# A decoder layer on one core: 32 of 44 feed-forward up steps as seven block products

## The reference

```python
D_MODEL = 1024; SEQ = 512; D_FF = 2816

def swiglu(x, w_gu, w_down):
    g, u = jnp.split(x @ w_gu, 2, axis=-1)
    return (jax.nn.silu(g) * u) @ w_down

def reference(x, ...):
    x = x + 0.5 * rms_norm(swiglu(rms_norm(x, ffn1_norm_pre), ffn1_w_gu, ffn1_w_down), ffn1_norm_post)
    h = rms_norm(x, mix_norm_pre)
    ...                                  # two attention mixers, gates, output projection
    x = x + rms_norm(merged @ w_out, mix_norm_post)
    x = x + 0.5 * rms_norm(swiglu(rms_norm(x, ffn2_norm_pre), ffn2_w_gu, ffn2_w_down), ffn2_norm_post)
```

## Time and profile before

| what | value |
|---|---|
| median of three executions | 1206.68 us (1205.62 to 1207.15) |
| the profiled execution | 1207.43 us, its span 1205.7 us |
| granted TensorE clock | 1.00, of full speed, in each of the 40 slices 0.9 or more |
| PE matmul busy | 1188.7 us, 99% of the span |
| PE weight loads busy | 986.2 us, 82% |
| DVE busy | 535.2 us, 44% |
| ACT busy | 399.0 us, 33% |
| POOL busy | 86.8 us, 7% |
| up steps (two feed-forwards) on the chain of waits | 53% with the gate and projection steps of the same line |
| down steps on the chain | 20% |

### The profile page before, as it was taken

The page is one execution under the profiler, slowest core; times in us unless marked ns, Lnnn a source line. Parts: engine busy times, 40 slices in busy tenths (PEclk is TensorE's granted clock), DMA queues, the critical chain, the costliest instruction groups (busy, mean ns, idle before and its releaser), DMA issues.

```text
span 1205.7 us, 15537 instructions
## 1 busy us (share of the span) xinstructions
PE 1188.7 (99%) x6054; PEld 986.2 (82%) x6054; DVE 535.2 (44%) x806; ACT 399.0 (33%) x643; POOL 86.8 (7%) x198
## 2 busy tenths in 40 slices
PE   9999999999999999999999999999999999999998
PEld 7888888888887888998777788887888888888886
DVE  3444444431226435436776343646444444442223
ACT  5222222221125211246676313325422222221113
POOL 7000000000005100000031100002000000000002
PEclk9999999999999999999999999999999999999999
DMA  7843333232225343371200232332333333333321
GB/s 207 263 113 96 104 104 87 87 123 105 105 87 145 96 118 104 108 242 36 73 3 2 70 105 70 123 105 70 101 90 88 104 104 96 83 115 107 105 70 70
DMA packets 138511, 123.19 MB, mean 102 GB/s; under 512 B 4180, under 2 KB 125180, under 8 KB 138444
## 3 DMA queue, kind: packets, MB, share of 16 engines
q1 hardware_dynamic: 134272, 108.02, 29.7%
q0 software_dynamic: 4080, 14.50, 3.7%
q10 hardware_dynamic: 112, 0.03, 0.0%
HBM read 118.08 MB, written 8.90 MB: 105 GB/s over the span
## 4 chain that ended last, share of the span: by engine, by line
PE 93%; DVE 2%; DMA 2%; ACT 1%; issue 1%; SPq 0%; DVEq 0%; ACTq 0%
PE ps L1369 53%; PE ps L1453 20%; PE ps L1556 4%; PE ps L1824 4%; PE ps L1622 2%; PE ps L1611 2%; DMA ring_raw<-in_ffn_w_gu 2%; PE ps L1808 2%; PE ps L1679 2%; PE ps L1657 1%; PE ps L1796 1%; PE ps L1393 1%; ACT ring_hi L670 1%; DVE ring_lo L946 1%; DMA x_tok<-in_x 0%
## 5 line engine op out<-in xcount | busy, mean ns | idle before, releaser
L1369 PE MATMUL ps<-xn_hi,ring_hi 128*128 128x512 f32 x992 | 388.7, 392 | 2.9 <-DVE ring_lo L946 1.6
L1369 PE MATMUL ps<-xn_hi,ring_lo 128*128 128x512 f32 x992 | 386.2, 389 | 0.0
L1369 PE MATMUL ps<-xn_lo,ring_hi 128*128 128x512 f32 x992 | 386.1, 389 | 0.0
L946 DVE TENSOR_TENSOR ring_lo<-ring_raw,ring_hi 128x2048 fp32r<-128x2048 f32 (+1 forms) x89 | 201.8, 2268 | 255.5 <-ACT ring_hi L670 255.5
L670 ACT ACTIVATE ring_hi<-ring_raw 128x2048 fp32r<-128x2048 f32 (+1 forms) x89 | 167.9, 1888 | 255.1 <-PE ps L1453 157.6
L1369 PEld LDWEIGHTS ps<-xn_hi,ring_hi 128*128 128x128 f32 x992 | 186.2, 188 | 42.7 <-issue 4.3
L1369 PEld LDWEIGHTS ps<-xn_hi,ring_lo 128*128 128x128 f32 x992 | 186.2, 188 | 39.1
L1369 PEld LDWEIGHTS ps<-xn_lo,ring_hi 128*128 128x128 f32 x992 | 186.3, 188 | 37.7
L1453 PE MATMUL ps<-ring_hi,hT_hi 128*128 128x512 f32 x352 | 136.9, 389 | 0.0
L1453 PE MATMUL ps<-ring_hi,hT_lo 128*128 128x512 f32 x352 | 136.9, 389 | 0.0
L1453 PE MATMUL ps<-ring_lo,hT_hi 128*128 128x512 f32 x352 | 136.9, 389 | 0.0
(11 more groups left out here) (232 smaller groups left out, 1161.6 us busy)
## 6 DMA issues: line engine op xcount, KB each, us to landing
ring_raw<-in_ffn_w_gu SPq DMA_DIRECT2D x86, 512.0 KB, 5.0
ring_raw<-in_ffn_w_down SPq DMA_DIRECT2D x44, 512.0 KB, 4.0
ring_raw<-in_w_in SPq DMA_DIRECT2D x44, 512.0 KB, 4.7
ring_raw<-in_w_out SPq DMA_DIRECT2D x8, 512.0 KB, 4.3
bias_rows_sparse<-bias_by_distance POOLq DMA_DIRECT2D x1, 2560.0 KB, 15.5
x_tok<-in_x SPq DMA_DIRECT2D x8, 256.0 KB, 5.3
ring_raw<-in_cmp_w_k SPq DMA_DIRECT2D x4, 512.0 KB, 4.4
ring_raw<-in_cmp_w_v SPq DMA_DIRECT2D x4, 512.0 KB, 4.5
```

Source lines behind the costliest of these rows:

```text
L946: e = dve.tensor_tensor(dst, src, f32(r), ALU.subtract)
L1369: e = pe.matmul(ps[:, 2 * (slot if pair is None else pair) + c, :], part(a, slot, k * 256 + c * P, P), xn[b][:, k, :], start=(k == 0 and i ...
```

## The change

In each feed-forward the first 6 up steps (`CLASSIC`) stay as they are. The other 16 (`MIXED`) are computed with Strassen's identity in Winograd's form: the weight step is four blocks B11, B12, B21, B22 (halves of K and the g and u columns), the normed x four blocks (halves of K and of the tokens), and seven block products take the place of eight. A block product is 4 slices of K x 3 matmuls of 128x128 by 128x256, 84 matmuls in a step instead of 48 of 128x512.

- **Weight side.** POOL forms four sums of blocks per step, 128x512 each: T3 = B22 - B12, T2 = T3 + B11, T1 = B12 - B11, T4 = B21 - T2 (`mix_weights`). ACT and DVE make high and low parts of seven blocks of 128x512 (`hi_block`, `lo_block`) instead of one of 128x2048, in the order B11, T2, T1, T3, B21, T4, B22. The slots are those of `ring_hi` and `ring_lo`, in 512-wide pieces; T1 and T4 are formed in the place of their own low parts.
- **x side**, once per feed-forward: POOL joins the high and low parts of x (`join_x`, four of 128x1024), DVE scales the four by `rb` (`norm_x`) and forms s1 and s3 (`mix_x`), POOL forms s2 and x12 - s2 (its own `mix_x`, called inside the first `mix_weights`, behind T3 and T2). ACT and DVE make seven high and low parts of 128x1024 (`hi_mixed`, `lo_mixed`). All of it stands between the steps 0 to 6 in the queues. The low part of x11 and of s1 may only be written when s2 has been formed.
- **Result side.** Three PSUM banks per step, alternately two sets, into which several products accumulate. ACT copies the first product to `s1`; DVE adds `s1` to the second bank after product 1 (`t_part`), after product 3 (`u_part`) and after product 5 (the u or g part of the second token half), and forms the other corners from them: 128x256 each. These sums stand ahead of the low parts that follow them in DVE's queue. PE waits for `t_part` before product 3, for `s1` before product 4, for `u_part` before product 5 and for the sum c22 before product 6.
- **h** is kept in fp32 (`hT`); its high part (`h_hi`, four slots) and low part, in the place of h itself, are made two steps of h at a time in the down stage (`hi_h`, `lo_h`, 128x1024), the first ones in the last two block steps.
- **POOL's queue.** The bias tables are built after the first feed-forward's up steps (`w_used` at 22) instead of at the start.

The diff, cut to its core:

```diff
+CLASSIC = 6
+MIXED = UP - CLASSIC
+SOURCES = ("B11", "T2", "T1", "T3", "B21", "T4", "B22")
...
+            def join_x(f):
+                pool.wait_ge(*xlo_event(2 * f, KD - 1))
+                for dst, ks, t0 in ((x_21[:, :, :], 0, 256), (x_22[:, :, :], 4, 256), (x_sum[0][:, :, :], 0, 0), (x_sum[4][:, :, :], 4, 0)):
...
+            def mix_weights(f, i, u, between=None):
...
+                pool.wait_ge(raw_loaded[u % 2], raw_count(f, i, u))
+                if not (isinstance(i, int) and 2 * i + u == 0):
+                    pool.wait_ge(blk_lo, of_step(f, i, u - 1, 6, 4))
+                pool.tensor_tensor(t3, b22, b12, ALU.subtract).then_inc(t_ready, 1)
+                pool.wait_ge(t_ready, of_step(f, i, u, 4, 1))
+                pool.tensor_tensor(t2, t3, b11, ALU.add).then_inc(t_ready, 1)
+                if between:
+                    between()
+                pool.wait_ge(*block_free(f, i, u, 2))
+                pool.tensor_tensor(t_sum(f, 2), b12, b11, ALU.subtract).then_inc(t_ready, 1)
+                pool.wait_ge(*block_free(f, i, u, 5))
+                pool.wait_ge(t_ready, of_step(f, i, u, 4, 2))
+                pool.tensor_tensor(t_sum(f, 5), b21, t2, ALU.subtract).then_inc(t_ready, 1)
...
+                mix_weights(f, 0, 0, lambda: mix_x(f))
...
+                def lo_mixed(b):
+                    if b in (0, 2):
+                        dve.wait_ge(x_mixed2, 2 * f + 1)
...
+                def mixed(i, u, last=False, late=lambda: None):
...
+                    dve.wait_ge(blk_used, of_step(f, i, u, 6, 2))
+                    dve.wait_ge(s1_ready, of_step(f, i, u, 1, 1))
+                    dve.tensor_tensor(t_part[:, :], y, s1[:, v, :], ALU.add).then_inc(t_taken, 1)
+                    late()
+                    for b in range(2):
+                        following(b)
...
+                    dve.tensor_tensor(u_part[:, :], y, s1[:, v, :], ALU.add).then_inc(u_taken, 1)
+                    dve.wait_ge(u_taken, of_step(f, i, u, 1, 1))
+                    dve.tensor_tensor(h_f32[:, v, 256:512], z, u_part[:, :], ALU.add).then_inc(c22_taken, 1)
...
+                    for b in range(2, 5):
+                        following(b)
...
+                    dve.tensor_tensor(hT[:, at_j], silu_g[:, v, :], h_f32[:, v, :], ALU.mult).then_inc(h_ready, 1)
+                    for b in (5, 6):
+                        following(b)
...
+                        if b == 3:
+                            pe.wait_ge(t_taken, of_step(f, i, u, 1, 1))
...
+                        for k in range(4):
+                            for q, (a, x) in enumerate(MODES):
+                                e = pe.matmul(ps[:, bank, 0:256], block_at(a, f, b)[:, k * P:(k + 1) * P], (x_hi, x_lo)[x][b][:, k, :],
```

More of the change, by code:

```diff
@@ new lines, in mix @@
+            def mix(f):
+                join_x(f)
+                mix_weights(f, 0, 0, lambda: mix_x(f))
+                mix_weights(f, 0, 1)
+                with pool.Fori(1, MIXED // 2) as i:
+                    for u in range(2):
+                        mix_weights(f, i, u)
+                pool.wait_ge(up_scaled, CLASSIC * (f + 1))
+            mix(0)
+            load_gain(g1_post)
+            pool.wait_ge(w_used, UP)
+            pool.memset(bias_vec[0:20, :], MASKED).then_inc(vec_filled, 1)
@@ L742, in ffn, with rest @@
                     root()
-                for u in range(2):
-                    up(0, u)
-                with act.Fori(1, UP // 2) as i:
-                    for u in range(2):
-                        up(i, u)
-                n = base + UP + 2
-                hi(0, n)
-                with act.Fori(0, (DOWN - 3) // 2) as i:
-                    for u in range(1, 3):
-                        hi(i, n + u)
+                for n in range(2):
+                    silu(n)
+                hi(0, base + 3)
+                for b in (3, 0, 2):
+                    hi_mixed(b)
+                silu(2)
+                hi(0, base + 4)
+                for b in (1, 4):
+                    hi_mixed(b)
+                silu(3)
+                hi(0, base + 5)
+                silu(4)
+                for b in range(4):
+                    hi_block(0, 0, b)
+                silu(5)
+                hi_block(0, 0, 4)
+                hi_mixed(5)
+                def rest():
+                    hi_block(0, 0, 5)
+                    hi_mixed(6)
+                    hi_block(0, 0, 6)
+                mixed(0, 0, late=rest)
+                mixed(0, 1)
+                with act.Fori(1, MIXED // 2 - 1) as i:
+                    for u in range(2):
+                        mixed(i, u)
+                mixed(MIXED // 2 - 1, 0, late=lambda: hi_h(0))
+                mixed(MIXED // 2 - 1, 1, last=True)
+                hi_h(1)
+                hi(0, first_down + 1)
+                for n in (2, 3):
+                    hi_h(n)
+                for n in range(2, DOWN):
+                    hi(0, first_down + n)
+                    if n + 2 < DOWN:
+                        hi_h(n + 2)
                 warm_root()
@@ L1140, in _ @@
                 if MIX + step + 2 <= GATE:
[L1141 removed]
+                    lo_halves(MIX + step + 2, step + 5)
                 if kind == "v":
@@ L1444, in down @@
                     pe.wait_ge(lo_ready, n0 + 1)
-                    for t in (2, 3, 0, 1) if n == 0 else range(NT):
-                        if n == 0 and t == 0:
-                            pe.wait_ge(up_scaled, h0 + UP)
+                    pe.wait_ge(hlo_ready, DOWN * f + n + 1)
+                    for t in (3, 0, 2, 1) if n == 0 else range(NT):
+                        if n == 0 and t in (0, 2):
+                            pe.wait_ge(h_ready, UP * f + UP - (1 if t == 0 else 0))
                         for c in range(2):
@@ L1458, in down @@
                     e.then_inc(w_used, 1)
+                for n in range(CLASSIC):
+                    up(n)
                 for u in range(2):
-                    up(0, u)
-                with pe.Fori(1, UP // 2) as i:
+                    mixed(0, u)
+                with pe.Fori(1, MIXED // 2) as i:
                     for u in range(2):
-                        up(i, u)
-                pe.wait_ge(hlo_ready, h0 + UP - 2)
-                for n in range(DOWN - 1):
+                        mixed(i, u)
+                for n in range(DOWN):
                     down(n)
-                pe.wait_ge(hlo_ready, h0 + UP)
-                down(DOWN - 1)
             pe.wait_ge(consts, 5)
```

359 lines of the change are left out of this document (276 added, 83 removed).

## The result

The changed kernel takes **1227.2 us** (median of 4 runs, 1226.2 to 1228.4) against 1206.9 for the kernel before: ratio 1.0168, 95% interval 1.0150 to 1.0186. It is slower, by 20 us, inside the range and 6 us above the predicted 1221. The profiled execution spans 1225.6 us.

The account below looks back on a forecast made before the run. PE's work was taken as the bound, 93% of the chain of waits. Terms -25.9 + 12.6 + 15.7 + 1.2 + 9.0 + 1.8 = +14.4 us on the median of 1206.7 gave 1221 us, range 1193 to 1239.

Parts of the forecast that it names:

- PE's own work: 32 up steps as 84 matmuls of 256 columns: 10.07 us against 10.88 a step, -25.9 us in all.
- Blocking between POOL and DVE: Operations reading SBUF on both engines exclude each other; 128x512 holds of 1.1 us (POOL) and 0.55 us (DVE).
- rival 3: Each operation blocks for its whole 1.28 or 0.69 us, PE 1.15 late a step: +19.6, 1241 us; chance 0.12.
- The steady step: Block steps 7 to 20: PE waits 0.45 us for t_part before product 3, 28 times, +12.6 us.
- The entry: Up step 5 starts 6.65 us late in the first feed-forward and 9.05 in the second: +15.7 us.
- L: End of DVE's low part 4 after up step 2's epilogue; PE can start step 5 at L + 21.35 us.
- Step 6: First block step: products 3 and 5 wait 3.5 + 1.0 us for late sums, +4.5 per feed-forward, +9.0.
- The joins: POOL's joins of x block DVE's low part of step 1, making PE 1.2 us late in the first feed-forward.
- Step 20: A low part of h in front of this step's low parts: +0.9 us per feed-forward, +1.8 in all.
- Rival 1: No POOL-DVE blocking that matters; only entry 10.7 and step 6 4.0 offset -25.9: 1195.5 us; chance 0.21.
- Rival 2: Blocking, but DVE goes ahead of T2 or POOL runs 0.3 us earlier; steady term 0: 1208.6 us; chance 0.13.
- Rival 4: The entry costs nothing because step 6's weights come early; the change gives its arithmetic: 1181 us; chance 0.06.

Follow-up runs that it names:

- run 9: run 8's order, with POOL adding only 8 of 128 columns per slice in its weight sums and zero-filling the rest: 1180.3 us (ratio 0.9779).
- run 2: Changed kernel with low parts 5 and 6 of a block step moved behind t_part in DVE's queue: 1227.2 us (ratio 1.017).
- run 6: run 4 with low parts 0 and 1 of the next step also moved behind u_part and c22 in DVE's queue: 1202.1 us (ratio 0.9955).
- run 7: run 6 with x's high and low part 5, h's low part 0 and POOL's joins of x also reordered: 1200.2 us (ratio 0.9945).
- run 8: run 7 with low part 6 also behind c22, and low part 4 behind t_part in up step 6: 1206.3 us (ratio 0.9993).
- run 1: Changed kernel with POOL forming s2 and x12 - s2 ahead of the first T3 and T2: 1206.9 us (ratio 1.0004).
- run 3: Changed kernel with POOL's four weight sums formed over 8 of 128 columns per slice, the rest zero-filled: 1202.0 us (ratio 0.9966).
- run 11: run 7's order with c21 moved ahead of low parts 3 and 4 in DVE's queue: 1188.9 us (ratio 0.985).
- run 10: run 8's order with c21 moved ahead of low parts 3 and 4 in DVE's queue: 1201.2 us (ratio 0.9949).
- run 4: Changed kernel with the edits of run 1 and run 2 together: 1207.2 us (ratio 1.0008).

## Why the prediction came out as it did

**PE's own work, -25.9: right.** Run 9 measures it directly: 32 steps in 322.7 us instead of 348.2 (32 x 10.88), -25.5. Its whole time is 26.6 below the kernel before; the rest is that the first matmul with weights starts earlier, by 1.0 us in the changed kernel (11.44 against 12.41) and by 1.6 in run 9, which no term had, and that the bias tables no longer stand at the start. For these I had given 0 to 0.5 and read their price as 0.19 from PE's idle time; from first matmul to first matmul, steps 3 and 4 took 11.24 and 11.00 before and step 3 takes 10.88 after, so it was 0.5.

**Blocking between POOL and DVE: right, in size too.** Predicted from two rows of before: a POOL 128x512 holds for 1.1, a DVE one for 0.55. Measured: a DVE low part that meets a starting POOL sum lasts 1.78 instead of 0.68, so 1.10, and a POOL sum that meets a DVE low part 1.81 instead of 1.29, so 0.52. The Trainium skill (SBUF — State Buffer, SBUF: two separate sides) says that whoever starts first gets the shared pair for the whole instruction; the trace shows 1.10 of 1.29 us, and rival 3, which took that to the letter, is out. The Trainium skill (SBUF — State Buffer, Who interferes with whom) says that a VectorE instruction with two SBUF inputs contends with a GpSimd one that reads SBUF and not with one that only writes; run 9 agrees: beside memsets of 128x480, 0.50 us each and four in a step, the low parts last 0.69 to 0.71 in the mean.

**The steady step, +12.6: right.** Predicted period 10.53, measured 10.53, with `t_part` 0.45 late in each. But I read the step as having one late place and much room behind it ("later in the step the order is kind"). Run 2 showed that it has not: `u_part` was about to be late as well, and runs 6 to 8 that what room there is depends on where the four holds of about 1.1 us fall in the ten.

**The entry, +15.7: right in cause and size, and one consequence missed.** From first matmul to first matmul, step 4 took 17.19 and 19.97 us instead of 10.88: step 5 came 6.3 late in the first feed-forward (predicted 6.65) and 9.1 in the second (9.05). From L to step 5 it was 21.1 and 21.6 (21.35). What no term of the sum had is what the pause does to PE's clock. After it step 5 took 12.81 and 13.42 us instead of 10.88, from its first matmul to that of step 6: in the first feed-forward the granted clock was 0.51 for 4 us, that is the 1.2 GHz level, with matmuls 0.43 us apart instead of 0.2267 until 81.1; in the second it was 0.50 for 5 us. The Trainium skill (TensorE: Matmul & The Clock Gate, Part 1: The HAM clock gate) gives 426.7 ns from start to start for 512 columns at the low level; the trace agrees with 430. That is 1.9 + 2.5 = **+4.5** (1.93 and 2.54), most of the 6 us between 1221 and 1227. The failed step is the move from "step 5 starts 6.65 late" to "so the end is 6.65 late": I priced a pause of PE at its own length. Run 1 confirms that it hangs on the pause: without it steps 2 to 5 take 10.88 each, and 20.3 us are gone, 15.4 of lateness, 4.5 of clock and 0.5 in the first step 6. The price is not fixed by the length of the pause: the six pauses before step 5 of the changed kernel and of runs 2 and 3 lost 5.0 to 9.1 us, and the step behind them was 1.7 to 3.0 longer, 3.0 and 1.7 in run 2 alone behind 6.2 and 9.1.

**Step 6, +4.5 each: 5.0 each.** Its first half was right (PE waits 3.3 for `t_part`; 3.5 predicted). The second half, 1.0 for product 5, did not show. Instead the clock was at the low level behind the first wait and the matmuls took 1.6 longer, and in the longer time `u_part` was ready. Run 1 shows both cases side by side behind equal waits of 3.27 us. First feed-forward, then second; the granted clock is the third number from the end of a row:

```profile
93.40:97.00 3.60, 3.56 (x30) 3.60 (x31) 2.90 (x6) 0.88 (x3) 1.52 (x1) 1.00 1.06 287
...
915.00:919.00 4.00, 4.00 (x27) 4.00 (x26) 3.78 (x8) 1.54 (x3) 0.00 (x0) 0.73 0.57 164
```

In the first the clock stayed up and product 5 waited 0.78; in the second it fell and product 5 did not wait. The first of these steps took 14.56 us, 4.5 more than 10.08, as predicted to the tenth; the second 15.05. The two costs nearly replace each other, so the term was 0.5 too small, not 1.6.

**The joins, +1.2: 1.3. Step 20, +1.8: 1.9** (0.95 each). Step 7 lost 0.6 each, which I had not counted: T3 waited 0.8 to 0.9 for its weights there.

**The sum** of what was measured, in the order PE's work, steady step, entry, clock behind it, joins, step 6, step 7, step 20: -25.5 + 12.6 + 15.4 + 4.5 + 1.3 + 10.0 + 1.2 + 1.9 = +21.4, less 1.0 for the earlier start and 0.5 for the bias tables, +19.9; the spans differ by 1225.6 - 1205.7 = 19.9.

**The rivals.** Rival 1 (no blocking) is out by the two lengths of DVE's low parts and by run 3. Its time of 1195.5 would have missed too: run 3, the nearest to a kernel without blocking, took 1202.0, with 12.7 us of pauses at the entry where it counted 10.7, and 5.4 of clock behind them where it counted none. Rival 2 (DVE's queue ahead by a little) is out for the changed kernel, where `t_part` is late in all 28 steps; steps of 10.08 beside full holds appear only with other orders, in part of run 6 and most of run 11. (Its time should have been 1208.4, not 1208.6.) Rival 4 is out by the pause before step 5; its time, 1181, is close to that of run 9 only because there both the entry and nearly all of POOL's reads were taken away.

## What to carry to other kernels

Where two engines keep each other out, count the holds of the whole period against the idle time of the waiting engine, and not only those in front of the operation that is late: here moving one late sum forward gave nothing, moving several things at once changed the block stage by anything between 0.8 us more and 4.2 less in four orders (runs 6, 7, 8 and 10), and took 8 to 9 us off it in a fifth (run 11). Pauses of TensorE of 5 to 9 us cost 1.7 to 3.0 us more than their length in these runs, so a stall at one place is worth more than it looks. And an operation that is put "in between" in one engine's queue (s2 behind T3) takes over all the waits of the one in front, here a weight DMA that waited for the engine it was to feed.

## What the runs showed of the hardware that I had not expected

- Equal waits of 3.27 us were followed by the low clock level in one feed-forward and not in the other of the same run (run 1). The same wait stands in step 6 of the changed kernel and of runs 2, 4 and 6, and the low level followed it there each time: nine times in ten. Behind the six pauses before step 5, 4.8 to 8.9 us of idle time, the clock was at the low level each time. In runs 7, 8, 10 and 11, whose longest wait in the block stage is 1.5 to 1.6 us, the granted clock never left the high level there.
- The same loop with the same order of instructions runs in different patterns within one execution (run 6): nine steps of 10.08 us in a row, or steps of 10.08 and of about 11.0 in turn. What differs between them is when POOL's sums meet DVE's queue; what throws it from one to the other was not tried. The two feed-forwards of one run differ (169.9 and 174.8).
